# Transposes of both heads' probabilities side by side in an attention layer: moving one transpose group and its copy in the order of two engines

## The reference, cut to what matters

```python
def dilated_attention_mixer(h, w_qkv, q_gain, k_gain, w_o, rel_bias):
    qkv = (h @ w_qkv).reshape(B, S, N_GROUPS, 3, ATTN_HEADS, ATTN_HEAD_DIM)
    for g, (window, dilation) in enumerate(DILATION_PAIRS):      # 3 groups
        q = rms_norm(qkv[:, :, g, 0], q_gain[g]) * scale
        k = rms_norm(qkv[:, :, g, 1], k_gain[g])
        v = qkv[:, :, g, 2]
        bias = band_bias(rel_bias[...], window, dilation)
        o, l = dilated_band_attention(q, k, v, bias, dilation)   # softmax(q k^T + bias) v, and log of its denominator
        ...
    weights = jax.nn.softmax(jnp.stack(lses), axis=0)
    o = jnp.sum(weights[..., None] * jnp.stack(outs), axis=0)
    return o.reshape(B, S, ATTN_HEADS * ATTN_HEAD_DIM) @ w_o
```

## Time and profile before

| | |
|---|---|
| Median of 3 runs | 1909.68 us (1909.13 to 1916.94) |
| The profiled execution's own time | 1909.68 us |
| Its span in the trace | 1907.9 us |
| TensorE busy | 1803.6 us, 95% of the span |
| VectorE, ScalarE, GpSimd busy | 926.7, 780.5, 203.9 us |
| Mean granted TensorE clock | 0.979 of full speed |
| Attention loop, `it` = 1 to 8 | about 998 to 1505 us of the span |

### The profile page before, as it was taken

One profiled execution on the slowest core, in us unless ns is written; L12 is line 12 of the kernel. 1 busy time (PEld: TensorE's weight loads), 2 busy tenths in 40 slices (PEclk: granted clock), 3 DMA queues, 4 the chain that ended last, 5 costly groups with the idle time before them and its releaser, 6 DMA issues.

```text
span 1907.9 us, 36430 instructions
## 1 busy us (share of the span) xinstructions
PE 1803.6 (95%) x15682; PEld 1401.8 (73%) x15682; DVE 926.7 (49%) x1585; ACT 780.5 (41%) x1326; POOL 203.9 (11%) x180
## 2 busy tenths in 40 slices
PE   8978999976699999999999999999999899999999
PEld 3745555555578888888888878878787688888887
DVE  6624555555444444433455555555655554444322
ACT  4333444444234222222446566656655542222211
POOL 0022333334110000000011111111111000000000
PEclk9998999998889999999999999999999899999999
DMA  3281010000223323333232222222222133333332
GB/s 122 78 252 44 28 31 30 31 28 6 71 67 100 100 88 100 100 99 100 84 104 78 84 72 79 78 78 75 81 67 78 44 93 99 97 100 99 100 94 94
DMA packets 57544, 155.04 MB, mean 81 GB/s; under 512 B 5591, under 2 KB 22535, under 8 KB 57384
## 3 DMA queue, kind: packets, MB, share of 16 engines
q1 hardware_dynamic: 57288, 152.63, 25.3%
q10 hardware_dynamic: 96, 0.07, 0.0%
HBM read 150.51 MB, written 11.61 MB: 85 GB/s over the span
## 4 chain that ended last, share of the span: by engine, by line
PE 68%; ACT 3%; DVE 1%; issue 1%; POOL 0%; ACTq 0%; DVEq 0%
PE bank L503 66%; PE bank L506 2%; ACT f L1433 2%; DVE f L1902 0%; ACT f L1420 0%; ACT f L1446 0%; ACT r L1411 0%; ACT f L1407 0%; ACT f L1438 0%; DVE f L1895 0%; POOL f L2048 0%; POOL f L2052 0%; POOL f L2050 0%; DVE r L1919 0%; DVE f L1913 0%
## 5 line engine op out<-in xcount | busy, mean ns | idle before, releaser
L503 PE MATMUL bank<-r 128*128 128x512 f32 x5616 | 1300.7, 392 | 7.3 <-DVE r L1919 3.7
L503 PEld LDWEIGHTS bank<-r 128*128 128x128 f32 x5616 | 1051.9, 188 | 238.6 <-issue 14.0
L503 PE MATMUL bank<-f 64*64 64x64 f32 (+6 forms) x9634 | 465.9, 256 | 83.9 <-DVE f L1640 16.8
L1509 DVE TENSOR_TENSOR r<-f,r 128x1024 fp32r<-128x1024 f32 x230 | 284.8, 1239 | 406.7 <-ACT r L1122 406.7
L503 PEld LDWEIGHTS bank<-f 64*64 64x64 f32 (+3 forms) x9634 | 301.2, 144 | 238.4 <-issue 112.6
L1122 ACT ACTIVATE r<-f 128x1024 fp32r<-128x1024 f32 x230 | 240.8, 1048 | 152.6 <-PE bank L503 138.1
L2077 POOL TENSOR_TENSOR r<-f,r 128x512 fp32r<-128x512 f32 x48 | 62.2, 1297 | 868.5 <-ACT r L1411 868.5
L1390 ACT ACTIVATE r<-f 128x512 fp32r<-128x512 f32 x44 | 27.8, 632 | 218.1 <-DVE f L1812 218.1
L1843 DVE TENSOR_TENSOR f<-bank,f 128x512 f32<-128x512 f32 x72 | 56.2, 780 | 73.0 <-PE bank L503 70.1
L1640 DVE TENSOR_TENSOR f<-bank,f 64x512 f32<-64x512 f32 x80 | 55.1, 689 | 63.9 <-PE bank L503 62.7
L506 PE MATMUL bank<-f 128*128 128x128 f32 x432 | 65.2, 281 | 9.9 <-DVE f L1902 8.4
(11 more groups left out here) (108 smaller groups left out, 966.6 us busy)
## 6 DMA issues: line engine op xcount, KB each, us to landing
f<-stream SPq DMA_DIRECT2D x247, 512.0 KB, 3.5
bias_copies<-bias_rows SPq DMA_DIRECT2D x3, 3072.0 KB, 25.1
f<-xT SPq DMA_DIRECT2D x16, 256.0 KB, 4.6
f<-lora_out SPq DMA_DIRECT2D x16, 128.0 KB, 3.9
f<-bias_copies SPq DMA_DIRECT2D x16, 128.0 KB, 3.1
f<-bias_copies SPq DMA_DIRECT2D x32, 64.0 KB, 2.9
outT<-f SPq DMA_DIRECT2D x8, 256.0 KB, 4.4
f<-const SPq DMA_DIRECT2D x1, 576.0 KB, 3.9
```

Of the source, the lines that this page charges most:

```text
L503: return nc.tensor.matmul(out, lhsT, rhs, start=start, stop=stop, skip_group_check=True)
L1509: TT(r(O_WLO + q % PAN * 1024, 1024), f(O_RAW + panel_of(q) % RAW * 1024, 1024), rf(O_WHI + q % PAN * 1024, 1024), ALU.subtract).then_inc( ...
```

## The change

In slots 3 to 6 the transposes of head 0 move ahead of `projection_aux`, and those of head 1 from behind logits or attend to just behind `projection_aux`. On ScalarE both copies stand in a row behind `split_high` and ahead of the aux instructions, and slot 5's exception is gone. No instruction is added or removed, and the waits that each step makes stay the same.

```diff
@@ TensorE's loop @@
                     if it == i == 0:
                         norm_sum(2)
+                    if a >= 0 and 3 <= i <= 6:
+                        flip_probs(a, 0, i - 3)
                     if i and it < NHP:
                         projection_aux(it, i - 1)
                     if a < 0:
@@
                     if i == 0:
                         projection_aux(a, 8)
                     if 3 <= i <= 6:
-                        flip_probs(a, 0, i - 3)
+                        flip_probs(a, 1, i - 3)
                     if i < 4:
                         logits(a, i)
                     if 4 <= i <= 7:
                         attend(a, i - 4)
-                    if 3 <= i <= 6:
-                        flip_probs(a, 1, i - 3)
@@ ScalarE's loop @@
                 for i in range(9):
-                    if it < NHP and i != 5:
+                    if it < NHP:
                         split_high(p_of(T_QKV + 9 * it + i) + LEAD)
                     if a >= 0 and 3 <= i <= 6:
                         keep_flipped(a, 0, i - 3)
-                    if it < NHP and i == 5:
-                        split_high(p_of(T_QKV + 9 * it + i) + LEAD)
-                    if i and it < NHP:
-                        projection_aux(it, i - 1)
-                    if a >= 0 and 3 <= i <= 6:
                         keep_flipped(a, 1, i - 3)
                     if it < NHP:
+                        if i:
+                            projection_aux(it, i - 1)
                         squares(it, i)
```

## The result

The changed kernel is slower: median 1933.38 us (1930.52 to 1936.12, 4 runs) against 1909.41 us (1908.30 to 1916.94, 4 runs), a ratio of 1.0117 with a 95% interval of 1.0087 to 1.0147. The forecast was 1923.8 us in a range of 1916 to 1931. The direction and the place were right; the time is 24 us over before's, not 14, and lies outside the range. Its profiled execution took 1931.57 us, with a span of 1929.8 us, 21.9 us more than before's.

The account below looks back on a forecast made before the run. TensorE in the attention loop was taken to bound the kernel. Waits of 1.98 us per iteration, seven times 13.9 us, plus 0.2 for the last iteration, added 14.1 to 1909.7 us: 1923.8 us, range 1916 to 1931.

Parts of the forecast that it names:

- What bounds the kernel: Attention loop: TensorE, busy 448.96 of 454.00 us at clock 1.00, so what it loses there is lost for the kernel.
- The spacing between the groups: Slots 3 to 6: start of head 0's transposes to start of head 1's, 1.30 us, or 1.07 for groups of three.
- What covers it now: Aux work between the groups hides part of the copy; 0.34 us stays bare in slots 3 and 6, 0.19 in slot 4.
- Slots 4 and 5 over ScalarE: ScalarE's order, not VectorE, ends slot 5's wait; loss 1.30 us, 0.19 in slot 4 and 1.11 in slot 5.
- F1: The transposes of head 1 on TensorE, which may start once head 0's copy is done; in slot 5 forecast at X + 10.72.
- X: The end of slot 4's product, the zero from which the times of slots 4 and 5 are counted.
- Some 0.2 us would go: Slot 5: had its exception been kept, probabilities would set F1 and some 0.2 us of the 1.30 us loss would go.
- The sum of the loop: Slots 3, 4 with 5, and 6: 0.34 + 1.30 + 0.34 = 1.98 us per iteration, seven times 13.9 us.
- The last iteration: No aux or product there; exponentials about 0.5 us earlier, bare attend matmuls in slot 5: +0.2 us, between -0.7 and +1.5.
- The clock rival: Slot 5's wait of about 1.5 us lowers the clock: 11 us if in all seven iterations, so 1935 us; chance 0.10.
- The range: Whole kernel: 1916 to 1931 us, from the low end of enough cover to the middle of the clock's case.

Follow-up runs that it names:

- the projection chunk: The kernel of before with one projection chunk per iteration moved into the recurrence's gap, where TensorE waits for ScalarE: 1924.72 us, ratio 1.0074.

## Why the prediction was right or wrong

- *What bounds the kernel*: right. TensorE in the attention loop, clock at 1.00, the added waits are paid nearly in full.
- *The spacing between the groups*, 1.30 us (1.07 for groups of three): right. After shows 1.29 (1235.75 to 1237.04) and 1.07 (1244.30 to 1245.37).
- *What covers it now*: this is the step that failed in the loop. For slot 3 I took 0.96 us of cover, the distance from the first of eight transposes to the logits. That distance holds 0.14 to 0.17 us that TensorE takes to go from transposes to logits or attend matmuls. Four transposes ahead of a product take 0.41 us in before (1225.95 to 1226.36), and ahead of logits 0.58 us in after (1237.04 to 1237.62). The wait ahead of them is not the reason, since behind the wait of before's slot 5 they take 0.38 us up to the product. In the new order the transposes ahead of the wait are followed by transposes, and those behind it by logits, so this switch hides nothing and is paid bare. The terms of slots 3 and 6 were 0.34 us each and measured 0.49 and 0.51.
- *Slots 4 and 5 over ScalarE*: right as a mechanism. F1 of slot 5 was forecast at X + 10.72 and came at X + 10.65 (1244.30 to 1254.95), behind `split_high` and the copy. The term was 1.30 us and measured 1.43, through the same switch: I counted 0.38 us from F1 to the attend matmuls, the time up to a product, and it took 0.59 (1254.95 to 1255.54). In slot 4 the three transposes also take 0.48 us up to attend and took 0.30 up to the product, but that runs beside ScalarE's path and only shortens TensorE's wait in slot 5. "Some 0.2 us would go" with the exception kept was 0.12. The wait of slot 5 shows as 1.26 us where I wrote about 1.5.
- *The sum of the loop*: over seven iterations the three terms are 3.2 us too small, of the 3.4 us by which the loop (17.3 us) exceeds its forecast (13.9 us).
- *The last iteration*, +0.2 us: the whole rest of the span took 0.2 us more. The exponentials came 0.38 us earlier than in before, for 0.5 forecast. But slot 5 there has two waits on VectorE, 3.15 and 1.18 us, and behind them the iteration was 1.1 us late (20.94 us from its logits to the six matmuls behind slot 5, where before took 19.82); most of that came back further on. That the sum met is luck.
- *The clock rival*: it did not happen in the loop. Waits of 1.26 us there left the mean clock at 1.00. The Trainium skill ("TensorE: Matmul & The Clock Gate", on the second failure mode, PSUM-queue cycling) tells of a kernel whose clock went back and forth under short idle spells between matmul groups. The trace of this loop does not show that, with idle spells of 0.25, 1.26 and 0.25 us in each 70.8 us.
- *The range*: it failed through something that none of its terms held. I put the stages ahead of the loop at nothing, from one execution (1909.7 us; 51 runs have a mean of 1911.8 and reach 1918.0), while the start of the loop moves by 12 us from run to run. Of the 24.0 us between the two medians of the comparison, 17.4 lie in the loop and behind it and some 6.6 ahead of it. With nothing ahead of it the time would have been 1926.8 us, inside the range; the loop's own error did not leave it. How far the first comparison came out was bad luck: over all runs the means are 1911.8 and 1931.1 us, of which 1.9 us lie ahead of the loop, and even 1931.1 is a hair over the upper bound.

What is shown: the bare copy, with the switch behind it, makes the loss (on TensorE head 1's move alone costs 3.02 us, head 0's alone -0.11 and both 1.65 us per iteration), and ScalarE's order adds 0.82 us through slot 5. That the clock moves the stage ahead of the loop is shown by equal stretches of the profiles; for the spread over all runs it rests on the correlation. Not shown: why the switch takes its 0.17 us, and whether any of the last 1.9 us belongs to the change.

## What to carry to other kernels

Two groups that share one bank need something between them that lasts as long as the copy out; moving work from between them to behind them costs the part of the copy that comes out bare, plus a switch of shapes, and on an engine that was busy for 99% of the stage little of it came back. A distance read between two rows can hold such a switch: before using it as cover, look at what followed the row there and what will follow it in the new order. Where a wait has two releases of nearly the same time, taking one away uncovers the other, so read both before pricing an order. When most of the time lies ahead of the place of a change, look at how much that part moves between runs before setting a range. And a copy that stands behind something else in ScalarE's list is late for TensorE wherever TensorE's matching step is put, as the projection chunk showed.

## What the runs showed of the hardware

A switch on TensorE from 128x128 transposes to logits or attend matmuls of 64 rows or columns took 0.17 to 0.18 us beyond the transposes' own time, four times per iteration (0.58 against 0.41 us for four, 0.48 against 0.30 us for three). Cutting a product of 24 matmuls to put four transposes inside cost about 0.1 us: the six, four and eighteen rows above run on without idle time and take 6.06 us (1246.55 to 1252.61, the next transposes), where the four transposes and the whole product of before take 5.95 (1242.19 to 1248.14). And runs of one and the same kernel, each on one core, spread over 12 us, or 0.6%, with mean granted clocks from 0.970 to 0.979, and the same 1064 matmuls of the recurrence took 45.27 us at a clock of 1.00 and 51.13 at 0.86: a difference of half a per cent needs a dozen runs here, or the profile, cut at a row that both kernels have.
